# Hybrid decoder layer on one core: finer first loads, another order of projections and compressions, split middle experts and a third slot for gate weights

## What is computed

```python
def _hier_moe(x, ...):                # 4 groups of 4 experts, top-1 group, top-2 experts
    ...
    for e in range(N_EXPERTS):
        h = jax.nn.silu(xt @ w_gate[e]) * (xt @ w_up[e])
        y = y + combine[:, e:e + 1] * (h @ w_down[e])
...
p = _rms(x, norm1_g) @ w_in           # columns: q, kvc, kvs, kvw, gates, u, v
q, kvc, kvs, kvw, gates, u, v = _split_proj(p)
# sparse attention: blocks compressed by _compress, selected blocks, sliding window
# _compress: h = gelu(einsum('bnckf,cfh->bnckh', x, w1)); einsum('bnckh,che->bncke', h, w2)
# x of the samples comes from cache pages, gathered by page_table
# gmlp(u, v); x = x + rms(concat) @ w_out
x = x + _hier_moe(_rms(x, norm2_g), ...)
y = _rms(x, final_norm_g)
```

## Time and profile before

| | |
|---|---|
| median of 3 runs | 773.23 us (772.24 to 773.83) |
| profiled execution | 771.26 us, its span 769.5 us |
| TensorE matmul busy | 703.3 us, 91% of the span |
| VectorE, ScalarE, GpSimd busy | 256.1, 183.0, 141.6 us |
| moved by DMA | 187.09 MB, mean 243 GB/s |
| mean granted TensorE clock | 0.963 |
| chain that ended last | PE 77%, DMA 10%, DVE 6%, ACT 3%, issue 3% |

### The profile page before, as it was taken

How to read it: one execution, slowest core, us unless ns; L and a number is a source line. 1 busy time by engine, 2 the same in 40 slices (tenths; PEclk the granted TensorE clock), 3 DMA queues, 4 the chain that set the end, 5 groups by cost and what they waited for, 6 DMA issues and landing times.

```text
span 769.5 us, 13681 instructions
## 1 busy us (share of the span) xinstructions
PE 703.3 (91%) x4940; PEld 477.1 (62%) x4940; DVE 256.1 (33%) x796; ACT 183.0 (24%) x461; POOL 141.6 (18%) x227
## 2 busy tenths in 40 slices
PE   4999999999997888999999789999999999998981
PEld 2485598658554555575555589877785867665640
DVE  4165302147347557751436631101101110101116
ACT  3111103021327744663212110010001011000114
POOL 0405034400440853000002010101111121110000
PEclk9999999999999998999999769999999999999995
DMA  9977245514783746014922627899999999999944
GB/s 333 381 270 233 70 137 198 189 45 179 245 293 122 209 134 208 1 56 141 417 110 97 253 79 251 306 328 367 365 370 357 381 393 380 385 378 399 372 130 165
DMA packets 53885, 187.09 MB, mean 243 GB/s; under 512 B 8561, under 2 KB 30354, under 8 KB 47154
## 3 DMA queue, kind: packets, MB, share of 16 engines
q1 hardware_dynamic: 41458, 151.49, 52.5%
q0 software_dynamic: 12064, 33.60, 14.5%
q10 hardware_dynamic: 288, 1.05, 0.4%
HBM read 172.97 MB, written 14.58 MB: 244 GB/s over the span
## 4 chain that ended last, share of the span: by engine, by line
PE 77%; DMA 10%; DVE 6%; ACT 3%; issue 3%; SPq 1%; DVEq 0%; POOL 0%; ACTq 0%
PE pb L569 71%; DMA ring<-in_w_up_dram 4%; PE pb L817 2%; PE pb L1086 2%; DMA ring<-in_cmp_pages_dram 1%; DMA x_rows<-xr 1%; DMA ring<-in_w_out_dram 1%; DMA ring<-in_w_in_dram 1%; SPq L378 1%; DVE xr L2328 1%; PE pb L844 1%; DMA ugr<-h_rows,qbd 1%; ACT tabs L1366 0%; DMA xr<-x_rows 0%; PE pb L720 0%
## 5 line engine op out<-in xcount | busy, mean ns | idle before, releaser
L569 PE MATMUL pb<-ring,xr 128*128 128x512 f32 (+3 forms) x640 | 138.4, 413 | 9.6 <-DMA ring<-in_w_in_dram 9.6
L569 PE MATMUL pb<-vnr,ring 128*128 128x96 f32 (+1 forms) x1152 | 132.8, 278 | 2.3 <-DVE vnr L2214 2.3
L569 PEld LDWEIGHTS pb<-vnr,ring 128*128 128x128 f32 x1152 | 132.1, 195 | 3.4 <-DVE vnr L2214 2.9
L569 PEld LDWEIGHTS pb<-ring,xr 128*128 128x128 f32 (+1 forms) x640 | 68.1, 151 | 72.1 <-issue 58.6
L569 PE MATMUL pb<-ring,qT 128*64 128x512 f32 (+2 forms) x256 | 90.8, 603 | 4.2 <-issue 3.7
L569 PE MATMUL pb<-ring,work 128*32 128x128 f32 (+2 forms) x512 | 71.6, 371 | 2.5 <-DMA ring<-in_w_out_dram 1.6
L378 POOL DMA_DIRECT2D ring<-in_sel_pages_dram x96 | 51.4, 536 | 93.3 <-issue 56.6
L2214 DVE COPY vnr<-pb 128x256 f32<-128x256 f32 (+2 forms) x16 | 8.5, 532 | 177.6 <-PE pb L1086 177.6
L569 PEld LDWEIGHTS pb<-ring,qT 128*64 128x64 f32 (+2 forms) x256 | 32.4, 160 | 51.2 <-issue 50.0
L2444 POOL DMA_INDIRECT x_rows<-kvn,qbd x15 | 22.3, 1485 | 227.2 <-DVE kvn L2242 96.5
L569 PE MATMUL pb<-ring 128*128 128x128 f32 (+1 forms) x512 | 59.6, 279 | 0.1
(11 more groups left out here) (356 smaller groups left out, 701.6 us busy)
## 6 DMA issues: line engine op xcount, KB each, us to landing
ring<-in_w_gate_dram SPq DMA_DIRECT2D x16, 2048.0 KB, 17.2
ring<-in_w_up_dram SPq DMA_DIRECT2D x16, 2048.0 KB, 21.3
ring<-in_w_down_dram SPq DMA_DIRECT2D x16, 2048.0 KB, 21.6
ring<-in_cmp_pages_dram SPq DMA_DIRECT2D x64, 128.0 KB, 5.2
ring<-in_cmp_pages_dram POOLq DMA_DIRECT2D x64, 128.0 KB, 5.4
ring<-in_w_in_dram SPq DMA_DIRECT2D x3, 2048.0 KB, 8.8
ring<-in_w_dram SPq DMA_DIRECT2D x1, 4096.0 KB, 19.7
ring<-in_win_dram SPq DMA_DIRECT2D x2, 2048.0 KB, 9.2
```

What stands on the lines that cost most here:

```text
L569: return nc.tensor.matmul(out, lhsT, rhs, start=start, stop=stop)
```

## The change

- x and the query weights are loaded in five pieces (k = 0; 1; 2, 3; 4, 5; 6, 7), each with its own semaphore. The KC weights are loaded right behind them.
- TensorE's first stage runs k outermost over the four prompt tiles with four banks; the sum of squares comes before k = 6. VectorE adds squares between the scalings.
- The sequence becomes: queries and KC together, compress(0), KW of the four prompt tiles, compress(1), KW of the sample tile and two v tiles, compress(2), the rest of v, compress(3). The orders on ScalarE, VectorE and GpSimd follow it.
- Middle experts (96 rows): 64 rows as a light expert and the other 32 in four groups of 32 array columns, for gate, up and down; `h_middle` is transposed; evictions of the result are three per engine.
- Gate weights rotate over three slots, the third in `xr`, which is free once `x2` has been stored; gate(n) waits for the gate product of n - 3.
- The rest is names of semaphores and copies of the slot weights to the partitions that the split experts read (`slot_w_high`, `slot_w_rest`).

```diff
+        hT_middle = qf[:, 0:384]
+        sg_middle = qf[:, 1024:1408]
+        h_middle = kwT[:, 0:384]
+        gate_slots = (ring[:, 2, :], ring[:, 4, :], xr[:, 0:SLOT])
...
+        PIECES = ((0, 1), (1, 2), (2, 4), (4, 6), (6, 8))
+        PIECE_OF = (0, 1, 2, 2, 3, 3, 4, 4)
...
+            if n in (PT, TILES):
+                return pb[7 if n == PT else 4]
...
+        def turn_bank(t):
+            return pb[5 + t % 2 if t < TILES else 4 + (t + 1) % 2]
...
-            for h in range(0, KD, KD // 2):
-                load(xr[:, h * TOK:(h + KD // 2) * TOK], t["xT"][:, h * TOK:(h + KD // 2) * TOK], "x_in%d" % (h > 0))
-                load(wv[:, h:h + KD // 2, :], ..., "wv_in%d" % (h > 0))
+            for n, (k, end) in enumerate(PIECES):
+                load(xr[:, k * TOK:end * TOK], t["xT"][:, k * TOK:end * TOK], "first_in%d" % n)
+                load(wv[:, k:end, :], ..., "first_in%d" % n)
+            w_in(BLK_KC)
...
+            def gate_in_turn(e, n):
+                after(sp, "g_mm", n - 2)
+                load(gate_slots[n % 3], slab("w_gate", e), "wg_in%d" % (n % 3))
...
+            sp.wait_ge(sem("x2_out"), 16 * (TILES + 1))
             sp.wait_ge(sem("experts_placed"), 1)
...
-            gate_up(placed[2], 2, 0, 1)
+            gate_in_turn(placed[2], 2)
+            up(placed[2], 2, 0, 1)
             for n in range(FIXED + 1, E):
                 if n == E - 1:
                     down(placed[n - 1], n - 1, (n - 1) % 2, (n - 1) // 2)
-                gate_up(placed[n], n, n % 2, n // 2)
+                gate_in_turn(placed[n], n)
+                up(placed[n], n, n % 2, n // 2)
                 if n < E - 1:
                     down(placed[n - 1], n - 1, (n - 1) % 2, (n - 1) // 2)
...
@@ TensorE @@
-            project(0)
-            project(1)
-            te.wait_ge(sem("ss_ready"), 1)
...
+            for k in range(KD):
+                if k == KD - 2:
+                    te.wait_ge(sem("ss_ready"), 1)
...
+                te.wait_ge(sem("first_in%d" % PIECE_OF[k]), 32)
+                te.wait_ge(sem("xg_ready"), k + 1)
+                for i in range(PT):
+                    ins = mm(pb[i][:, :], xT[:, k, i * P:i * P + P], wq[:, k, :], k == 0, k == KD - 1)
...
+            project(PT)
+            project(TILES)
+            turned(0)
+            turned(1)
+            project(TILES + 1)
+            turned(2)
+            turned(3)
+            project(TILES + 2)
+            turned(4)
+            for n in range(TILES + 3, 2 * TILES):
+                turned(n - 3)
                 project(n)
+            for n in range(2 * TILES - 3, 2 * TILES):
+                turned(n)
             compress(0)
+            for n in range(2 * TILES, 3 * TILES - 1):
                 project(n)
+                if n == 2 * TILES + 1:
                     position_bias()
                 if n > 2 * TILES:
                     turned(n - 1)
+            compress(1)
+            project(3 * TILES - 1)
+            turned(3 * TILES - 2)
+            project(3 * TILES)
             turned(3 * TILES - 1)
+            project(3 * TILES + 1)
             compress(2)
+            for n in range(3 * TILES + 2, 4 * TILES):
                 project(n)
             compress(3)
...
+            def middle_gate_up(n):
...
+                    for k in range(KD):
+                        for q in range(2):
+                            mm(pb[bank][64 * q:64 * q + 64, 0:256], xeT[0][:, k, 0:64],
+                               wv[:, k, 256 * q:256 * q + 256], k == 0, k == KD - 1)
+                    for k in range(KD):
+                        for q in range(4):
+                            ins = mm(pb[bank][32 * q:32 * q + REST, 256:384], xeT[0][:, k, 64:MIDDLE_CAP],
+                                     wv[:, k, 128 * q:128 * q + 128], k == 0, k == KD - 1)
+            def middle_turned(n):
...
+                for c in range(3):
+                    ins = nc.tensor.transpose(pb[5][:, P * c:P * c + P], h_middle[:, P * c:P * c + P], ident)
+            def middle_down(n):
...
+                for f in range(FE):
+                    q, c = divmod(f, 2)
+                    for d in range(2):
+                        ins = mm(pb[4][64 * d:64 * d + 64, :], hT_middle[:, P * c + 64 * q:P * c + 64 * q + 64],
+                                 wv[:, f, W * d:W * d + W], f == 0, f == FE - 1)
+                for f in range(FE):
+                    for d in range(4):
+                        ins = mm(pb[5][32 * d:32 * d + REST, 0:256], hT_middle[:, 256 + 32 * f:256 + 32 * f + REST],
+                                 wv[:, f, 256 * d:256 * d + 256], f == 0, f == FE - 1)
...
@@ VectorE @@
-            for t in range(TILES):
+            for t in range(2 * TILES):
                 turned(t)
             position_bias()
...
@@ GpSimd @@
             half_pages(0)
-            half_pages(1)
             for i in range(TILES):
                 po.wait_ge(sem("proj_out"), BLK_KC * TILES + i + 1)
                 ...
-            half_pages(2)
+            half_pages(1)
             for i in range(TILES):
                 ...
                 po.wait_ge(sem("proj_out"), BLK_KW * TILES + i + 1)
                 ...
+            half_pages(2)
             half_pages(3)
```

More of the change, by code:

```diff
@@ L330, in after, with is_split, split_before @@
                 eng.wait_ge(sem(name), value)
-        def light_before(n):
-            return sum(is_light(m) for m in range(n))
+        def is_split(n):
+            return cap_of(n) < CAP
+        def split_before(n):
+            return sum(is_split(m) for m in range(n))
         def expert_units(b, first, eng, last, ahead=None):
@@ L1095, in gate_up @@
                     te.wait_ge(sem("hl_ready"), light_done)
-                for slots, bank, weights, done in ((WG, 2, "wg_in", "g_mm"), (WU, 3, "wu_in", "u_mm")):
-                    te.wait_ge(sem(weights + "%d" % par), 16 * (turn + 1))
-                    wv = ring[:, slots[par], :].rearrange("p (k f) -> p k f", k=KD)
+                for bank, done in ((2, "g_mm"), (3, "u_mm")):
+                    if bank == 3:
+                        te.wait_ge(sem("wu_in%d" % par), 16 * (turn + 1))
+                        weights = ring[:, WU[par], :]
+                    elif in_turn:
+                        te.wait_ge(sem("wg_in%d" % (n % 3)), 16 * (n // 3 + 1))
+                        weights = gate_slots[n % 3]
+                    else:
+                        te.wait_ge(sem("wg_in%d" % par), 16 * (turn - E // 2 + len(range(par, E, 3)) + 1))
+                        weights = ring[:, WG[par], :]
+                    wv = weights.rearrange("p (k f) -> p k f", k=KD)
                     for f in range(FE):
@@ L1118, in light_gate_up @@
                 te.wait_ge(sem("xt_ready"), 2 * n + 2)
-                te.wait_ge(sem("h_ready"), n)
-                for slots, bank, weights, done in ((WG, 2, "wg_in", "g_mm"), (WU, 3, "wu_in", "u_mm")):
-                    te.wait_ge(sem(weights + "1"), 16 * (n // 2 + 1))
-                    wv = ring[:, slots[1], :].rearrange("p (k f) -> p k f", k=KD)
+                if is_split(n - 1):
+                    te.wait_ge(sem("hl_ready"), split_before(n))
+                else:
+                    te.wait_ge(sem("h_ready"), n)
+                for bank, done in ((2, "g_mm"), (3, "u_mm")):
+                    if bank == 2:
+                        te.wait_ge(sem("wg_in%d" % (n % 3)), 16 * (n // 3 + 1))
+                        weights = gate_slots[n % 3]
+                    else:
+                        te.wait_ge(sem("wu_in1"), 16 * (n // 2 + 1))
+                        weights = ring[:, WU[1], :]
+                    wv = weights.rearrange("p (k f) -> p k f", k=KD)
                     for k in range(KD):
@@ L1166, in last_of @@
                     light_down(n)
+                elif is_split(n):
+                    middle_down(n)
                 else:
@@ L1383, in _ @@
             act.wait_ge(sem("rs_ready"), 1)
-            for n in range(TILES + 2):
+            for n in range(2 * TILES):
+                projected(n)
+            act.wait_ge(sem("gates_zero"), 1)
+            for n in range(2 * TILES, 2 * TILES + 2):
                 projected(n)
@@ L1617, in _ @@
                 V.tensor_scalar(xT[:, k, :], xT[:, k, :], vec[:, k:k + 1], None, ALU.mult).then_inc(sem("xg_ready"), 1)
-            for k in range(1, KD):
-                link(V.tensor_tensor(sq[0], sq[0], sq[k], ALU.add))
+                if k >= 1:
+                    link(V.tensor_tensor(sq[0], sq[0], sq[k], ALU.add))
             dve.sem_inc(sem("ss_ready"), 1)
@@ L1676, in _ @@
             dve.wait_ge(sem("cst_in"), 16)
-            for t in range(TILES):
+            for t in range(2 * TILES):
                 turned(t)
             position_bias()
-            for t in range(TILES, 3 * TILES):
+            for t in range(2 * TILES, 3 * TILES):
                 turned(t)
```

171 lines of the change are left out of this document (108 added, 63 removed).

## The result

The changed kernel takes 778.73 us (median of 11 runs, 775.77 to 781.26); the kernel before took 773.57 us beside it (11 runs, 769.65 to 776.03). The ratio is 1.0071 (95%: 1.0052 to 1.0089): slower by 5.2 us by the medians and 5.5 by the ratio, where 3.1 had been forecast. The profiled execution took 780.24 us, with a span of 778.5 us and a mean granted clock of 0.943.

The account below looks back on a forecast made before the run. The DMA engines were taken as the slower party since about 515 us, with TensorE living on advance loads. First stage +7.2 us and end -4.1 us summed to +3.1, giving 776.3 us; range 764 to 785.

Parts of the forecast that it names:

- The start: First stage: with five pieces TensorE starts at 6.35 us (-3.3 us) and the 0.69 us wait goes; together -4.0 us.
- The short waits: First stage: three new short waits against one of 1.19 us, net +1.0 us; a 1.30 us wait goes, -1.3 us.
- GpSimd's queue: First stage: third batch's page numbers and loads come behind a store; TensorE waits 9.0 us (7 to 11) before compression 2.
- The restart: First stage, after the pause before compression 2: TensorE restarts at a lower granted clock, +1.3 us (0 to 2).
- The split: Expert stage: 64 and 32 rows save TensorE 4.2 us a middle expert, 21 us for five; the saving becomes waiting.
- The third slot: Expert stage: gate loads issued 3 to 7 us earlier, costed at 0 (-5.4 us if one slab comes forward).
- The end: Last down product begins at its weights' landing, gaining 5.6 us less 1.5 for expert 14's add: -4.1 us (-6 to +2).
- TensorE as the bound: Expert stage: DMA could deliver faster with a deeper queue, so the split's 21 us come out: 759.4 us; chance 0.10.
- Late pages that don't stall: First stage: reading page numbers overlaps the wait for the store, so 10.3 us fall away: 766.0 us; chance 0.12.
- The clock in the expert stage: TensorE's clock falls through waits on DMA; last up and down products take twice as long: 783.5 us; chance 0.13.
- The split that doesn't do what it says: Expert stage: four 32-column products don't run together, gate and up products take 6.9 us more each: over 800; chance 0.05.
- The signs: Trace checks, among them: start near 6.4 us, 9 us idle before compression 2, landings 38 us a pair, middle products near 11.

Follow-up runs that it names:

- two pieces: Changed kernel with x and the query weights in two pieces again, k still outermost: 783.55 us, ratio 1.0127.
- the numbers ahead: Changed kernel; GpSimd reads its third compression's page numbers before waiting for the last window-key rows, still issuing the loads behind the store: 770.33 us, ratio 0.9978.
- the experts alone: Kernel before with only the expert part of the change (split middle experts, third gate slot), first stage untouched: 770.19 us, ratio 0.9962.
- the half loads: From the seventh expert on, only half of each weight slab loaded: changed kernel 756.78 us (0.9805), kernel before 765.05 us (0.9896).
- all gates ahead: Changed kernel with GpSimd's page loads early and each gate load issued ahead of the previous expert's up load: 767.78 us, ratio 0.9936.
- the early gates: Changed kernel, GpSimd's page loads early, only gates of experts 3, 4, 5 put ahead: 764.87 us (0.9902); same order on the experts alone: 766.87 us (0.9918).

## Why the prediction was right, point by point

**The start: right.** 6.52 us against 6.35 (the parts that the forecast names add up to only 6.2); the wait for the second half is gone. In the run with two pieces a later start of 4.5 us arrived at the end as 4.3 to 4.8.

**The short waits: right.** The three new ones are 0.55, 0.99 and 1.83 us; with the 1.19 of the earlier trace rows and a wait of 1.12 us before the last key transpose (at 93.46 us in the kernel before), which the last one replaces, taken off, the net is +1.06 (forecast +1.0). The 1.30 us of the earlier trace rows is gone. The position bias costs 0.45 us, not 0.85. What was missed is a wait of 0.90 us at 109.14 for page loads of compression 1; in the other profiles with the new order it was anything from nothing to 2.1 us.

**GpSimd's queue: right, and shown.** 8.21 us against 9.0. Two runs took only this away and brought the time down by 7 to 8 us (by the ratios). The run with the numbers ahead narrows it to the 8.87 us of reading numbers: without them 1.60 us of the wait are left. The prediction had put reading and issuing on the path as one sum, which was right for the changed kernel.

**The restart: mis-sized.** Forecast +1.3 us (0 to 2), measured 17.47 - 14.56 = +2.9. The granted clock was 0.74 in the stretch from 140 to 160 us. The value had been taken from the first start of the kernel, where only some 1.4 us were lost. In the five profiles with the pause the half compression took 16.36, 16.44, 16.45, 17.05 and 17.47 us, so the price is 1.8 to 2.9; in the four profiles of the new order without the pause the same half takes 14.53 to 14.56.

**First stage in sum.** -3.1 - 0.7 + 1.1 - 1.3 + 0.45 + 0.9 + 8.2 + 2.9 = +8.4 us, measured +9.8 (forecast +7.2). The allowance of 0.4 for compression 3 wasn't needed. The 1.4 us that are left are spread over small gaps and the slower first products; no run singles them out.

**The split: right.** 11.05 and 5.52 us per product, as summed from the narrow products of the earlier trace rows (11.0 and 5.6); the transposes are 0.55, not 0.4. And it is right that the stage hides most of it: 38.4 us a pair, waits for weights from 622 us on, and with whole loads the split is worth some 3 to 5 us (3.2 and 2.9 by the ratios of the runs without it and with it alone, 4.9 and 5.2 in the stage), where 19.4 were at stake.

**The third slot: right.** 0 forecast, ratio 1.0074 without and 1.0071 with. The lower bound of -5.4 us was for the case that a slab is brought forward. With SP's order changed so that three gates go ahead, 4.8 and 3.4 us came out (by the ratios, on the two first stages); how much of that needs the third slot no run shows.

**The end: the size right, in part by luck.** -4.1 forecast. The expert stage gave -4.9 in this profile and -5.2 with the experts alone, by the medians of that run -2.7. The forecast was that the last down product moves up to its weights' landing (-5.6) and that the landing comes 1.5 us later. Neither came as told. Counted from the first transpose of gathered rows the last slab landed 284.8 us later before and 284.1 after, so not later but 0.7 earlier. And the product started 1.4 us behind the landing, released by VectorE: after its last wait for weights (at 709.07 us) TensorE had only its own work before it, and the first product of it took 7.21 us where the same one takes 5.52 at full clock. The two misses, 2.2 us and 1.4, cancel in the main, and the spread of the stage in single profiles (3.4 us) is larger than either.

**The sum.** +7.2 - 4.1 = +3.1 forecast, +9.8 - 4.9 = +4.9 in the two stages, +5.2 by the medians. In the first stage the forecast was 2.6 us short. The restart (1.6 us), the wait for pages that nobody had asked about (0.9), the 1.4 us that no term explains and a start that gave 0.2 less make more than that; GpSimd's wait, the position bias and compression 3, all forecast too high, take 1.6 off. The end gave 0.8 more than forecast and so hid part of the miss.

**The rivals.** TensorE as the bound (759.4): refuted by the half loads, which bring the pace from 38.4 to 29.4 us a pair. And the DMA engines deliver 358 to 399 GB/s in stretches of 20 us from 560 to 740 us, 381 in the mean, as before (368 to 392 from 560 to 720 us, 381 in the mean), though TensorE now waits for them. Late pages that don't stall (766.0): refuted by the stall of 8.21 us and by the two runs in which it goes. The clock in the expert stage (783.5): the granted clock was 0.91 in four stretches of 20 us between 620 and 720, where waits are, and 1.00 in the others from 560 to 740. Three light gate or up products took 5.2 to 5.4 us instead of 3.67. The last up and down products ran at full clock (3.65 us for the down product), so the rival is refuted as priced. But the slow product at 709 us lies behind the last wait for weights, and up to 1.4 us of it reached the end. The split that doesn't do what it says: refuted by 11.05 us (its price of 6.9 us a product has no working; three more times 1.95 us would be 5.85).

**The signs.** All came but two in part: TensorE's wait before compression 2 is put down by the profile to no releaser ("issue"), and it takes the two runs to tie it to GpSimd; and the last down product didn't start at its landing.

The trace also bears on the rule of the Trainium skill that was weighed ("DMA: Bandwidth & Descriptors", "Issuing engines are not separate DMA queues"). It counts the sequencer's time for initiating a DMA as usually small beside the DMA itself. Here 16 loads of 128 KB took 9.32 us to issue, and each landed 2.5 us after its issue (median), so that time wasn't small; yet alone it cost TensorE only 1.60 us. The 8.87 us of reading numbers, of which that sentence doesn't speak, made the rest of the stall.

## What to carry to other kernels

When an order of work is changed, follow every queue that keeps its own order, also that of the engine that only issues loads: numbers that are read to registers belong ahead of the wait, not behind it. Judge a stage by the growth of the landing times, not by a busy TensorE: where they grow, work taken from TensorE turns into waiting, and what pays is a slab moved to a time when the DMA engines have room. (That the order of use should be kept where they have none is argued from the waits of the run with all gates ahead; its time and that of the early gates, 0.9936 and 0.9902, have intervals that overlap.) And before a difference of 3 us between two single executions is explained, the same stage of a kernel that shares its code should be looked at.

## What the runs showed that was not expected

A pause of 8 us cost TensorE another 1.8 to 2.9 us in the products behind it, up to a third on top; in the profile shown the granted clock was 0.74 from 140 to 160 us, where it was 1.00 in the kernel before.

The attention stage, from compression 3 to the first transpose of gathered rows, has the same code in all the kernels here. It took 278.0 us in the profile of before, 281.5 in that of the changed kernel, and 278.3 to 281.6 in those of the eleven experiments. Part of it is the clock: TensorE's busy time for the same products is 2.5 us longer in the changed kernel's profile than in that of before (254.57 and 252.10 us, granted clock 0.94 and 0.95), and one group of four products at 236 to 247 us took 2.08 us in some profiles and 1.13 in others. The rest isn't explained. The expert stage spreads as much, 283.8 to 287.2 us in four profiles with the same code. This is as large as most of the effects that were to be measured, so that they had to be read from ratios over many runs, and a stage of one profile says little by itself.

Reading 16 numbers into registers took GpSimd 8.77 and 8.87 us in the two rows shown, some 0.55 us a number, nearly as long as issuing 16 DMAs (9.32 us).
